# LayerNorm chains of a one-core fp32 layer moved off GpSimd and cut by tile; twelve conditioning units moved behind w_o

## What is computed

```python
ada = (c @ w_ada + b_ada)[:, None, :]            # 9 sequences, 6 * 2048 columns
sh1, sc1, g1, sh2, sc2, g2 = jnp.split(ada, N_ADA, axis=-1)
mixed = (jax.nn.sigmoid(gate_p) * y_p + jax.nn.sigmoid(gate_c) * y_c) @ w_o
x = _layernorm(ALPHA * x + g1 * mixed, ln1_g, ln1_b)
u2 = x * (1 + sc2) + sh2
h = jnp.square(jax.nn.relu(u2 @ w_ff1 + b_ff1))  # 2048 -> 8192
x = _layernorm(ALPHA * x + g2 * (h @ w_ff2 + b_ff2), ln2_g, ln2_b)
```

## Time and profile before

| | us |
|---|---|
| median of 3 runs (1519.34 to 1521.69) | 1519.38 |
| the profiled execution | 1519.79 |
| its span, from first to last instruction | 1518.0 |

### The profile page before, as it was taken

How to read it: one execution, slowest core, us unless ns; L and a number is a source line. 1 busy time by engine, 2 the same in 40 slices (tenths; PEclk the granted TensorE clock), 3 DMA queues, 4 the chain that set the end, 5 groups by cost and what they waited for, 6 DMA issues and landing times.

```text
span 1518.0 us, 28596 instructions
## 1 busy us (share of the span) xinstructions
PE 1464.7 (96%) x11843; PEld 1371.2 (90%) x11843; DVE 854.5 (56%) x984; ACT 521.2 (34%) x343; POOL 91.1 (6%) x73
## 2 busy tenths in 40 slices
PE   6999999999999999999599999999999999999994
PEld 3788898898888889899599999999999999999994
DVE  0556556556679565547855454545445545445567
ACT  0323222323334323323543433443334433334342
POOL 0000000000180000002420000000000000000002
PEclk9999999999999999999799999999999999999997
DMA  9988888888885986795265556555556555655531
GB/s 338 346 296 299 309 305 302 291 318 297 301 291 191 351 303 243 276 329 166 84 176 184 181 179 179 180 184 175 185 174 188 173 192 168 190 171 191 168 109 57
DMA packets 172836, 343.09 MB, mean 226 GB/s; under 512 B 5757, under 2 KB 7181, under 8 KB 172766
## 3 DMA queue, kind: packets, MB, share of 16 engines
q1 hardware_dynamic: 172422, 341.28, 66.1%
q0 software_dynamic: 368, 1.18, 0.3%
HBM read 340.15 MB, written 2.79 MB: 226 GB/s over the span
## 4 chain that ended last, share of the span: by engine, by line
PE 91%; DVE 4%; SPq 2%; DMA 2%; DVEq 0%; issue 0%; ACT 0%; ACTq 0%
PE main L1031 29%; PE main L1032 28%; PE main L1033 28%; PE ps_ada L1062 5%; DMA ada_raw<-in_w_ada 2%; DVE w_lo L654 1%; SPq L309 1%; DVE PB L735 0%; PE ps_adat L1113 0%; SPq L295 0%; DVE PB L747 0%; DVE G L921 0%; DVE Uf L916 0%; PE main L1275 0%; SPq L283 0%
## 5 line engine op out<-in xcount | busy, mean ns | idle before, releaser
L654 DVE TENSOR_TENSOR w_lo<-raw,w_hi 128x2048 fp32r<-128x2048 f32 (+1 forms) x228 | 520.8, 2285 | 492.3 <-ACT w_hi L486 492.0
L486 ACT ACTIVATE w_hi<-raw 128x2048 fp32r<-128x2048 f32 (+1 forms) x228 | 431.6, 1893 | 908.8 <-PE main L1033 908.8
L1031 PE MATMUL main<-U,w_hi 128*128 128x264 f32 (+1 forms) x2320 | 662.1, 285 | 15.5 <-DVE U L955 12.8
L1033 PE MATMUL main<-U,w_lo 128*128 128x264 f32 (+1 forms) x2320 | 659.3, 284 | 0.0
L1032 PE MATMUL main<-U,w_hi 128*128 128x264 f32 (+1 forms) x2192 | 620.6, 283 | 0.0
L1031 PEld LDWEIGHTS main<-U,w_hi 128*128 128x128 f32 x2320 | 437.2, 188 | 49.6 <-issue 44.0
L1033 PEld LDWEIGHTS main<-U,w_lo 128*128 128x128 f32 x2320 | 436.4, 188 | 0.0
L1032 PEld LDWEIGHTS main<-U,w_hi 128*128 128x128 f32 x2192 | 413.2, 189 | 0.0
L1031 PE MATMUL main<-H,w_hi 128*128 128x264 f32 x1280 | 365.1, 285 | 0.0
L1033 PE MATMUL main<-H,w_lo 128*128 128x264 f32 x1280 | 362.2, 283 | 0.0
L1032 PE MATMUL main<-H,w_hi 128*128 128x264 f32 x1152 | 327.3, 284 | 0.0
(11 more groups left out here) (175 smaller groups left out, 532.2 us busy)
## 6 DMA issues: line engine op xcount, KB each, us to landing
raw<-in_w_ff SPq DMA_DIRECT2D x128, 1024.0 KB, 5.2
ada_raw<-in_w_ada SPq DMA_DIRECT2D x88, 1024.0 KB, 6.9
raw<-in_w_in SPq DMA_DIRECT2D x64, 1024.0 KB, 9.9
raw<-in_w_o SPq DMA_DIRECT2D x16, 1024.0 KB, 9.6
raw<-in_w_pool_up SPq DMA_DIRECT2D x8, 1024.0 KB, 9.2
raw<-in_w_conv_up SPq DMA_DIRECT2D x8, 1024.0 KB, 10.8
PB<-in_w_ada SPq DMA_DIRECT2D x4, 1024.0 KB, 10.7
G<-in_w_ada SPq DMA_DIRECT2D x4, 1024.0 KB, 15.5
```

Source lines behind the costliest of these rows:

```text
L486: nc.scalar.activation(w_hi[:, s % HL, 0:size], raw[:, s, 0:size], ACT.Copy).then_inc(hi_ready, 1)
L654: tt(w_lo[:, s % HL, 0:size], raw[:, s, 0:size], w_hi[:, s % HL, 0:size].bitcast(F32), ALU.subtract).then_inc(unit_split, 1)
L1031: mm(out, wh, x_hi, start=start, stop=False)
L1033: return mm(out, wl, x_hi, start=False, stop=stop)
```

## The change

- **Conditioning.** The 12 units of w_o leave it. SP puts 4 of their loads between the second and third w_o block, 6 behind the loads of the first FF block, 2 behind one more FF load; they go to seven places that are free then (`gap_slot`). PE runs 2 units before `norm(0)`'s matmuls, 4 behind them, 3 before the second unit of FF block 0 and 3 before its third. `ada_turn` comes after that block.
- **LayerNorm.** POOL subtracts nothing any more. DVE subtracts the guess from tiles 12 to 15 ahead of time too and adds the gated output to that (`last_gated`), tile by tile; ACT squares them one by one. PE sums the mean of the last four in `ps_adat`, which then holds the offset itself. All tiles get the offset subtracted from G (`less_off`), on DVE. The square-root table is loaded before the last squares.
- **U.** The 8 sample columns of all tiles are done at once (`sample_u2`). Tiles 0 to 3 come one by one, the others in fours. The first unit of every FF1 block runs chunk by chunk over the four banks (`first_chunks`).
- POOL makes `u2_coef` during w_o, and the residual's coefficients only when the last conditioning rows are there.

The core of the diff (empty lines left out):

```diff
+        gap_slot = [ada_u[:, 0], ada_u[:, 1], eight_tiles(Uf, 0), eight_tiles(PB, 8),
+                    eight_tiles(PB, 16), eight_tiles(PB, 24), eight_tiles(PB, 0)]
+        gap_slot += [gap_slot[k] for k in (0, 1, 3, 4, 5)]
+        gap_after = {7: 0, 8: 1, 9: 3, 10: 4, 11: 5}
...
+            def load_gap(k):
+                if k in gap_after:
+                    sp.wait_ge(ada_used, gap_used(gap_after[k]))
+                elif k < 2:
+                    sp.wait_ge(ada_used, gap_used(-1))
+                elif k < GAP_HELD:
+                    sp.wait_ge(part_done, done(U_WO - 1))
+                else:
+                    sp.wait_ge(part_done, done(U_FF - 1))
+                col = (GA2 + 4 + k // ADA_UNITS * 4) * P
+                sp.dma_start(gap_slot[k], w_ada[k % ADA_UNITS][:, :, col:col + UC]).then_inc(gap_landed[k], 16)
...
+            load_wo(0)
+            load_wo(1)
+            for k in range(GAP_HELD):
+                load_gap(k)
+            load_wo(2)
+            load_wo(3)
+            for j in range(4):
+                load_ff1(0, 0, j)
+            for k in range(GAP_HELD, GAP_ADA - 2):
+                load_gap(k)
+            load_ff1(0, 1, 0)
+            for k in range(GAP_ADA - 2, GAP_ADA):
+                load_gap(k)
+            for j in range(1, 4):
+                load_ff1(0, 1, j)
...
-            def minus_mean(l):
-                pool.wait_ge(mu_ready, l + 1)
-                pool.wait_ge(ln_sq, 4 * l + 4)
-                for c in range(1, 4):
-                    t4 = slice(4 * c, 4 * c + 4)
-                    g_tt(G[:, t4, :], X[:, t4, :], mu.unsqueeze(1).to_broadcast([P, 4, TOK]),
-                         ALU.subtract).then_inc(ln_centred, 1)
-            minus_mean(0)
...
+            def last_squares(l):
+                act.wait_ge(u2_coef, 1)
+                nc.scalar.activation(hist_sum[:, 0, 0:1], ones[:, 0:1], ACT.Sqrt)
+                for t in range(NT - MT, NT):
+                    act.wait_ge(ln_d, LN_D * l + 3 + t - (NT - MT) + 1)
+                    nc.scalar.activation(G[:, NT + t, :], G[:, t, :], ACT.Square).then_inc(ln_sq, 1)
...
+            for t in range(KC):
+                act.wait_ge(ln_norm, t + 1)
+                scale_u2(t)
                 act.drain()
-                nc.scalar.copy(U[:, 8 * c:8 * c + n, :], Uf[:, 8 * c + 4:8 * c + 4 + n, :]).then_inc(u2_hi_ready, 1)
+                nc.scalar.copy(U[:, t, :], Uf[:, KC + t, :]).then_inc(u2_hi_ready, 1)
+            for c in range(1, 4):
+                if c > 1:
+                    hi_part(c, 25, U_FF + c)
+                act.wait_ge(ln_norm, KC + c)
+                for t in range(4 * c, 4 * c + 4):
+                    scale_u2(t)
+                act.drain()
+                nc.scalar.copy(U[:, 8 * c:8 * c + 4, :], Uf[:, 8 * c + 4:8 * c + 8, :]).then_inc(u2_hi_ready, 1)
...
+            def last_gated(n, gate):
+                dve.drain()
+                for m in range(MT):
+                    t = NT - MT + m
+                    gt = ada[:, gate + t, :]
+                    dve.wait_ge(part_done, done(n, m))
+                    tt(small[:, m, :], bank[m][:, PROMPT:TOK], gt[:, 1:SEQS], ALU.mult)
+                    stt(G[:, t, 0:PROMPT], bank[m][:, 0:PROMPT], gt[:, 0:1], G[:, t, 0:PROMPT],
+                        ALU.mult, ALU.add).then_inc(psum_free, 1)
+                    dve.drain()
+                    tt(G[:, t, PROMPT:TOK], G[:, t, PROMPT:TOK], small[:, m, :], ALU.add).then_inc(ln_d, 1)
+                    if m in (1, 2):
+                        dve.drain()
+                        r = tt(last_sum, last_sum if m == 2 else G[:, t - 1, :], G[:, t, :], ALU.add)
+                r.then_inc(ln_in, 1)
...
-                dve.drain()
-                minus_guess(3)
-                pairs(NT - MT)
-                tt(last_sum, pair[:, 0, :], pair[:, 1, :], ALU.add).then_inc(ln_in, 1)
-                dve.wait_ge(ln_sq, 4 * l + 4)
-                sq = G[:, 2 * NT - 4:2 * NT, :]
-                tt(sq[:, 0:2], sq[:, 0:2], sq[:, 2:4], ALU.add)
-                dve.drain()
-                tt(G[:, NT + 1, :], sq[:, 0], sq[:, 1], ALU.add).then_inc(ln_sums, 1)
+                sq = G[:, 2 * NT - MT:2 * NT, :]
+                for k in (0, 2):
+                    dve.wait_ge(ln_sq, LN_D * l + 3 + k + 2)
+                    tt(sq[:, k, :], sq[:, k, :], sq[:, k + 1, :], ALU.add).then_inc(ln_sums, 1)
                 dve.wait_ge(ln_mean, 2 * l + 2)
-                tt(mu, early_mean, ps_ada[:, 0:TOK], ALU.add)
-                dve.drain()
-                tt(off, mu, guess, ALU.subtract).then_inc(mu_ready, 1)
-                dve.drain()
-                tt(off, off, off, ALU.mult)
+                cp(off, ps_adat[:, 0:TOK])
+                dve.drain()
+                tt(off_sq, off, off, ALU.mult)
                 dve.drain()
                 dve.wait_ge(ln_moment, l + 1)
-                stt(var, ps_b[:, 0:TOK], EPS, off, ALU.add, ALU.subtract).then_inc(ln_var, 1)
-                tt(G[:, 0:4, :], X[:, 0:4, :], mu.unsqueeze(1).to_broadcast([P, 4, TOK]), ALU.subtract)
+                stt(var, ps_b[:, 0:TOK], EPS, off_sq, ALU.add, ALU.subtract).then_inc(ln_var, 1)
...
+            def less_off(t, n, cols):
+                w = cols.stop - cols.start
+                tt(G[:, t:t + n, cols], G[:, t:t + n, cols], off[:, cols].unsqueeze(1).to_broadcast([P, n, w]),
+                   ALU.subtract)
+            def normalise(t, n, cols):
+                w = cols.stop - cols.start
+                dve.drain()
+                return tt(G[:, t:t + n, cols], G[:, t:t + n, cols],
+                          rstd[:, cols].unsqueeze(1).to_broadcast([P, n, w]), ALU.mult)
...
                 early_norm(0, j)
-            add_gated(15 + U_WO, 12, GA1)
...
+                normalise(0, NT, sample)
...
+            def lo_u2(c, t, n):
+                dve.wait_ge(u2_hi_ready, c)
+                hi = t + t // KC * KC
+                tt(U[:, hi + KC:hi + KC + n, :], Uf[:, hi + KC:hi + KC + n, :], U[:, hi:hi + n, :].bitcast(F32),
+                   ALU.subtract).then_inc(u2_ready, 1)
...
             norm(0)
+            less_off(0, 1, prompt)
+            less_off(0, NT, sample)
+            finish_rstd(0)
             dve.wait_ge(u2_coef, 1)
...
+            dve.wait_ge(ada_used, gap_used(2))
+            sample_u2()
+            for t in range(KC):
+                if t:
+                    less_off(t, 1, prompt)
+                normalise(t, 1, prompt).then_inc(ln_norm, 1)
+                if t:
+                    lo_u2(t, t - 1, 1)
+            lo_u2(KC, KC - 1, 1)
+            for c in range(1, 4):
+                less_off(4 * c, 4, prompt)
+                if c > 1:
+                    lo_u2(KC + c - 1, 4 * c - 4, 4)
+                normalise(4 * c, 4, prompt).then_inc(ln_norm, 1)
+                lo_part(c, U_FF + c)
+            lo_u2(KC + 3, 12, 4)
+            dve.wait_ge(ada_used, gap_used(GAP_ADA - 1))
...
             norm(1)
+            less_off(0, 4, every)
+            finish_rstd(1)
             for c in range(4):
-                normalise(1, c).then_inc(ln_norm, 1)
+                if c:
+                    less_off(4 * c, 4, every)
+                normalise(4 * c, 4, every).then_inc(ln_norm, 1)
...
             def norm(l):
                 pe.wait_ge(ln_in, 2 * l + 2)
-                mm(ps_ada[:, 0:TOK], ones, last_sum, start=True, stop=True).then_inc(ln_mean, 1)
-                pe.wait_ge(ln_sums, 2 * l + 2)
-                mm(ps_b[:, 0:TOK], ones, G[:, NT + 1, :], start=False, stop=True).then_inc(ln_moment, 1)
+                mm(ps_adat[:, 0:TOK], ones, last_sum, start=True, stop=False)
+                pe.wait_ge(ln_d, LN_D * (l + 1))
+                mm(ps_adat[:, 0:TOK], ones, G[:, NT - 1, :], start=False, stop=True).then_inc(ln_mean, 1)
+                pe.wait_ge(ln_sums, 3 * l + 2)
+                mm(ps_b[:, 0:TOK], ones, G[:, 2 * NT - 4, :], start=False, stop=False)
+                pe.wait_ge(ln_sums, 3 * l + 3)
+                mm(ps_b[:, 0:TOK], ones, G[:, 2 * NT - 2, :], start=False, stop=True).then_inc(ln_moment, 1)
...
+                for k in range(first, first + count):
+                    pe.wait_ge(gap_landed[k], 16)
+                    if k == 0:
+                        pe.wait_ge(row_copied, G_WO)
+                    b, u = divmod(k, ADA_UNITS)
+                    four_chunks(u, gap_slot[k], b * SEQS, b == 0, b == 2).then_inc(ada_used, 1)
+                return first + count
+            at = gap_ada(0, GAP_FIRST)
             norm(0)
...
+            def first_chunks(n, t0):
+                pe.wait_ge(unit_split, split_done(n))
+                for c in range(KC):
+                    pe.wait_ge(u2_ready, c + 1)
+                    for m in range(MT):
+                        if c == 0:
+                            pe.wait_ge(psum_free, bank_free(t0 + m))
```

(14 more changed lines are left out.)

186 lines of the change are left out of this document (90 added, 96 removed).

## The result

| | before | after |
|---|---|---|
| median, device us | 1519.43 (4 runs, 1519.34 to 1521.69) | 1503.08 (4 runs, 1500.91 to 1503.68) |
| profiled execution, its span | 1519.79, 1518.0 | 1503.68, 1501.9 |
| mean granted clock | 0.985 | 0.991 |

The ratio is 0.9884, with a 95% interval of 0.9872 to 0.9896: 16.3 us faster, where 20.0 were forecast. The time lies in the range of the prediction, 3.7 us above its point. Later runs, in another job, gave a median of 1503.58 for the changed kernel (4 runs) against 1520.1 (6 runs), and ratio 0.9888 [0.9870, 0.9906]. A seventh run of the kernel before took 7531.95 us there, at a granted clock of 0.179, and is left out.

The account below looks back on a forecast made before the run. TensorE, busy 96% of the span, was taken to bound the kernel, short of work at the two LayerNorms. Savings of 12.3 + 2.3 + 5.4 = 20.0 us from 1519.4 gave 1499.4 us, range 1495.0 to 1506.0.

Parts of the forecast that it names:

- Pairs out of w_o: In w_o: removing six pairs of conditioning units, 2.05 us each, saves 12.3 us.
- a w_o unit above 5.9: In w_o: units were forecast 5.8 us apart; one above 5.9 would show the forecast wrong.
- From T on: From the end of the last w_o matmul through FF block 0: 44.2 us becomes 41.9, saving 2.3.
- the landing of the sixth load: First LayerNorm: the sixth moved conditioning unit's load lands 7.9 us after the last w_o matmul ends.
- the other of my signs of being wrong: Moved conditioning units: a TensorE wait over 1 us for a load of w_ada would show the forecast wrong.
- The last three units on the path: FF block 0, before its third unit: three conditioning units cover no wait and cost 3.0 us.
- The chunk order: All 16 FF1 blocks: running the first unit chunk by chunk, with 192 more bank changes, costs nothing.
- LayerNorm 2: Second LayerNorm to the last output issue: 26.3 us becomes 20.9, saving 5.4.
- Late loads: Rival, moved conditioning loads: the twelfth lands late, FF block 0 ends 4.5 us later, 1504 us; chance 0.12.
- Longer chain: Rival, first LayerNorm: slower handovers or small VectorE steps add 3 us, 1502 to 1503 us; chance 0.15.
- Half clock through the block: Rival, FF block 0: short waits keep TensorE at half clock throughout, 1522 us; chance 0.03.
- POOL change gives nothing: Rival, both LayerNorms: long VectorE operations keep their length without GpSimd, 2.3 us back at each, 1504 us; chance 0.02.

Follow-up runs that it names:

- e3: Changed kernel with GpSimd kept busy by three 1056-column subtractions at the first LayerNorm, result unaffected: 1506.69 us (one run).
- e2: Changed kernel with the chunk-by-chunk order only in the first FF1 block, the other 15 in the old order: 1500.92 us, ratio to before 0.9874.
- e5: Changed kernel with the matmuls of the twelve moved conditioning units left out, their loads and waits kept: 1501.55 us (one run).
- e1: Changed kernel with the twelve conditioning units put back into w_o in six pairs, both LayerNorm chains kept: 1512.98 us, ratio to before 0.9953.
- e9: Changed kernel with GpSimd kept busy by three four-tile subtractions at the second LayerNorm, on a buffer nobody reads: 1505.53 us.

## Why the prediction was right, and where it wasn't

- **Pairs out of w_o, 12.3.** The pairs gave 2.06 each, 12.4 (forecast 2.05 and 12.3). w_o alone shows 12.49, and 0.9 of it is the turn, which stands behind FF block 0 now and costs the same there, as forecast. Less that, w_o gave 11.6. The 0.7 that is missing is the split of its second unit, by which one step between the copies is 6.6 us long, where a w_o unit above 5.9 was to mean that I was wrong: I had called w_o's units PE's because FF's are, with the bound on the loads alone, and hadn't asked what DVE does at the start of w_o (it splits M there first). The loads themselves were never late.
- **From T on, 2.3.** It came out as 3.1 without the turn (2.30 with it). So this term is 0.8 too small where the one above is 0.7 too large, and that the two together are nearly right (14.8 against 14.6) is partly luck. Steps: tile 0 ready at T+10.2 (forecast T+10.4, though its own terms add up to T+10.2), first FF matmul T+11.2 (T+10.6), second unit T+20.8 (T+21.5), end of block 0 T+41.3 (T+41.9). The square of 0.43, the samples' 0.29 and the two 1.25s (1.22 and 1.23 measured) were right to a few hundredths, and e3 shows the first to be POOL's doing. The step that failed is the landing of the sixth load: T+9.3, not T+7.9, and a wait of PE of 2.62 us, the other of my signs of being wrong that came in. About 0.3 of the miss is in every profile; the rest comes by chance, for e2 to e5 have T+8.1 to T+8.3. It cost nothing in the end, because the split of tiles 4 to 7 and not the first unit sets the second (e1 and e5 show it at T+20.8 without any conditioning units between).
- **The last three units on the path, 3.0.** They took 2.8. That leaving all twelve out gains nothing (e5) wasn't foreseen: their price at PE and their worth for the clock cancelled.
- **The chunk order, nothing.** It costs 0.76 from copy 106 on (e2). My reason, that 48 matmuls with four changes of bank take 48 x 0.121, was too coarse to see it: 0.05 us a unit is 1% of it. It asked after the wrong thing, too, since the same changes of bank cost nothing behind an FF2 block.
- **LayerNorm 2, 5.4.** It gave 4.7. DVE's chain was as forecast (reciprocal V+4.1 against the V+4.4 named at the end, last group V+14.8 against V+15.0) and DVE's last copy came early, at V+18.6 instead of V+19.2. The mis-sized term is SP: I let its last issue follow DVE's last copy by 1.7, as before, and it came 2.9 behind. In the rows of both kernels the last nine issues stand back to back, from DVE's fourth copy on, and they took 4.2 us now and 3.9 before. By these rows only an earlier fourth copy would move the end; no run tried it.
- **What was not in the sum.** The terms of the change together make 18.8 where I had 20.0. The other 2.7 of the 3.9 between forecast and profile are the start (63.3 to 66.4 us to copy 3 over the twelve profiles: PE's waits for conditioning loads near 48 us are 1.2 us longer in this profile than in that of before, and the clock, at 0.50 behind them, comes back near 55.6 us and not near 52.8) and the clock near 457 us. Both vary between executions of one kernel. My range covered them only because it was made wide for other reasons; the narrower band, 2.5 us about the sum, to which I gave 0.60, missed, and the time lies where I expected late loads or a longer chain, neither of which happened.
- **The rivals.** Late loads: one was late by 1.4 us and hidden; the twelfth landed 1.7 late, and its unit ran at its place without a wait. Longer chain: no, the handovers came out shorter. Half clock through the block: it lasted under 4 us, and in the changed kernel every stretch from 725 us to the end of block 0 is at 1.00. By the rule of the Trainium skill, TensorE: Matmul & The Clock Gate, section "A second HAM failure mode: psum-queue depth-cycling", the short waits would have made the clock oscillate. In the changed kernel the trace doesn't agree: one fall, after 2.62 us of idleness, and none behind it. In e1 and e5, with 6.3 and about 3 us of idleness before two units in succession, it fell twice, but those are long waits, of which this rule doesn't speak. POOL change gives nothing: refuted by e3 and e9.

## What to carry to other kernels

Work moved off the path into a wait of PE is worth more than its own length if it shortens the idleness that PE's clock reacts to, and leaving such a filler out can gain nothing; price both. When another engine's operation looks too long for its shape, see who else is on SBUF at that moment: here a GpSimd operation of two inputs, for whose result nobody waited in e3, held four short VectorE operations for 4.1 us. And at the tail count the issues of the queue that stores the outputs, each with its gap to the one before; here nine of them back to back set the last 4 us.

## What the runs showed of the hardware

- The same wait of 2.3 us was followed by a fall of the granted clock in eight profiles and by none in four, the code being the same; each fall cost 1.5 us. A forecast to a microsecond must leave room for that.
- Stretches with the same code repeat to 0.01 to 0.02 us over 388 and 705 us, in different jobs. Differences of profiled stretches decided in one run what medians, of runs that spread over 2 to 4 us, can hardly tell.
- 48 matmuls that change the PSUM bank every 3 took 5.86 us behind an FF1 block and 5.81 behind an FF2 block; with a change every 12 they took 5.81 and 5.83. So the change of bank alone shows no price here.
- Of loads of 1 MB that were issued one behind the other, the second after T landed at T+8.1 to T+8.3 in five profiles and at T+9.0 to T+9.4 in four, the loads behind T being the same.
- DVE's operations of 8, 264 and 264 columns with both inputs in SBUF took 1.3, 0.75 each and 1.25 us longer beside GpSimd, the ones with a PSUM input none.
- An ACT operation of 256 columns that stood alone between others took 0.60 us; four in a row took 2.07, 0.52 each.
